# An expert stage rewritten as one flat list of passes, with a turning weight ring and sums kept in PSUM

## What is computed

```python
logits = xf @ w_router + b_router          # 256 tokens, 32 experts
top_v, top_i = lax.top_k(logits, 4)        # 4 experts per token
gates = softmax(top_v)
# for each expert e, on the rows xb of the tokens that chose it:
g = xb @ w_gate[e] + b_gate[e]
u = xb @ w_up[e] + b_up[e]
g = minimum(g, 7.0); u = clip(u, -7.0, 7.0)
glu = g * sigmoid(1.702 * g)
y = ((u + 1.0) * glu) @ w_down[e] + b_down[e]
out[token] += gate * y
# then x + out, and a final rms_norm
```

## Time and profile before

| | |
|---|---|
| time, median of 3 runs | 1571.98 us (1571.66 to 1572.05) |
| span of the profiled execution | 1570.4 us |
| TensorE busy | 1454.5 us, 93% |
| VectorE, ScalarE, GpSimd busy | 502.8, 185.6, 25.1 us |
| moved by DMA | 466 MB, 297 GB/s over the span |
| expert stage, first weight product to last | 546.2 to 1556.9 us |

### The profile page before, as it was taken

How to read it: one execution, slowest core, us unless ns; L and a number is a source line. 1 busy time by engine, 2 the same in 40 slices (tenths; PEclk the granted TensorE clock), 3 DMA queues, 4 the chain that set the end, 5 groups by cost and what they waited for, 6 DMA issues and landing times.

```text
span 1570.4 us, 17757 instructions
## 1 busy us (share of the span) xinstructions
PE 1454.5 (93%) x6407; PEld 656.1 (42%) x6408; DVE 502.8 (32%) x1092; ACT 185.6 (12%) x371; POOL 25.1 (2%) x26
## 2 busy tenths in 40 slices
PE   5999989997988899999999999999999999999896
PEld 4856567664664433333333333333333333333332
DVE  1425424434484421322322322322322322322222
ACT  1212011111160000100100100000000000000001
POOL 0000000001000100000000000000000000000000
PEclk9999989999998699999999999999999999999999
DMA  9722163233520662999999999999999999999291
GB/s 327 275 74 82 54 243 131 68 119 101 193 107 1 238 264 95 381 423 429 428 427 428 430 426 430 427 426 428 430 427 428 427 427 429 429 426 427 111 381 73
DMA packets 61683, 466.04 MB, mean 297 GB/s; under 512 B 6497, under 2 KB 10333, under 8 KB 36957
## 3 DMA queue, kind: packets, MB, share of 16 engines
q1 hardware_dynamic: 58152, 462.78, 71.9%
q0 software_dynamic: 624, 2.10, 0.4%
q10 hardware_dynamic: 2884, 0.87, 0.2%
HBM read 464.68 MB, written 1.05 MB: 297 GB/s over the span
## 4 chain that ended last, share of the span: by engine, by line
issue 79%; PE 17%; DVE 3%; ACT 1%; POOL 1%; DVEq 0%; POOLq 0%
PE bank L710 6%; PE bank L717 5%; PE bank L872 1%; PE bank L1047 1%; PE bank L965 0%; PE bank L918 0%; PE bank L1024 0%; POOL small L453 0%; ACT mem L643 0%; PE bank L1013 0%; PE bank L1060 0%; PE bank L943 0%; PE bank L766 0%; PE bank L788 0%; PE bank L722 0%
## 5 line engine op out<-in xcount | busy, mean ns | idle before, releaser
L1089 PE MATMUL bank<-ring,mem 128*64 128x512 f32 x3264 | 725.0, 596 | 25.1 <-ACT mem L685 22.0
L1089 PEld LDWEIGHTS bank<-ring,mem 128*64 128x64 f32 x3264 | 229.1, 137 | 469.6 <-issue 438.1
L1821 DVE TENSOR_SCALAR mem<-bank 128x512 f32<-128x512 f32 x34 | 23.5, 692 | 505.0 <-PE bank L1096 505.0
L710 PE MATMUL bank<-ring 128*128 128x256 f32 x768 | 168.6, 380 | 1.0 <-DVE ring L1526 1.0
L710 PEld LDWEIGHTS bank<-ring 128*128 128x128 f32 x768 | 145.1, 190 | 22.4 <-DVE ring L1526 1.4
L1833 DVE TENSOR_TENSOR x<-x,bank 128x512 f32<-128x512 f32 x140 | 89.3, 680 | 164.9 <-PE bank L1101 164.9
L717 PE MATMUL bank<-ring 128*128 128x512 f32 (+2 forms) x320 | 124.0, 549 | 3.1 <-DMA ring<-in_w_in_dram 2.0
L717 PEld LDWEIGHTS bank<-ring 128*128 128x128 f32 x320 | 63.3, 200 | 59.6 <-issue 53.0
L1101 PE MATMUL bank<-mem 64*128 64x512 f32 x280 | 78.5, 639 | 3.7 <-ACT mem L679 1.5
L681 ACT ACTIVATE mem<-mem 128x512 f32<-128x512 f32 x32 | 20.1, 629 | 511.9 <-DVE mem L1821 511.9
L1096 PE MATMUL bank<-const,mem 128*64 128x512 f32 x272 | 69.9, 592 | 0.0
(11 more groups left out here) (331 smaller groups left out, 842.5 us busy)
## 6 DMA issues: line engine op xcount, KB each, us to landing
ring<-in_w_gate_dram SPq DMA_DIRECT2D x64, 2048.0 KB, 14.2
ring<-in_w_up_dram SPq DMA_DIRECT2D x64, 2048.0 KB, 12.9
ring<-in_w_down_dram SPq DMA_DIRECT2D x64, 2048.0 KB, 9.0
ring<-in_w_in_dram SPq DMA_DIRECT2D x19, 2048.0 KB, 9.1
ring<-in_w_out_dram SPq DMA_DIRECT2D x6, 2048.0 KB, 7.8
ring<-in_w_in_dram SPq DMA_DIRECT2D x2, 1056.0 KB, 7.4
const<-in_consts_dram SPq DMA_DIRECT2D x1, 1872.0 KB, 7.3
x<-in_x_dram SPq DMA_DIRECT2D x1, 1024.0 KB, 5.2
```

What stands on the lines that cost most here:

```text
L710: i = mm(b[:, S * j:S * j + S], w[:, k, P * (c + j):P * (c + j + 1)], hT[:, k, :], start=(k == 0), stop=(k == KC - 1))
L1089: i = halves(lambda n, at: mm(dst[at, :], lhs[:, c, T * h:T * (h + 1)], w[:, c, 512 * n:512 * (n + 1)], start=(h == 0 and c == 0), stop=(d ...
L1821: i = ts(g_sb, GB[:, :], SWIGLU_LIMIT, None, ALU.min)
```

## The change

All passes are one list, numbered j = expert + extra passes so far. Tables by pass replace those by expert: `of_expert` (which expert pass j belongs to), `slot_at` (each token's place less 64 j) and `slot_gate`, computed before the stage by a few small matmuls. VectorE and ScalarE run one loop over the number of passes, read from `n_total`. TensorE runs over the experts in rounds of four, each with a body for passes that aren't the expert's last and one for the last; both call `expert_block`, and only the last gives slots back. The eight slots turn: load n goes to slot n % 8. Four banks (`OUT`) hold x and collect b_down and all results in PSUM until the end; x is put there by a matmul with the identity. The biases use 32 rows each (gate at partitions 0 to 31, up at 32 to 63) and come first in a pass. Gathered rows share a bank with the gate product, transposed rows with the up product, and h transposed with y.

```diff
-MAIN_STEPS, PRE_STEPS, EX_STEPS = 6, 1, 8
+BLOCK_STEPS = 4
+RING = SLOTS + 2
+RING_EXPERTS = 4
+MAX_BLOCKS = 48
...
-        DB = [bank[0], bank[2], bank[6], bank[7]]
-        GB, UB, YB, XS, XTB, HTB, OB = bank[0], bank[1], bank[2], bank[3], bank[4], bank[5], bank[6:8]
+        OUT = [bank[2], bank[3], bank[6], bank[7]]
+        GXS, UXT, YHT, GTB = bank[0], bank[1], bank[4], bank[5]
...
+            round_turns = RING_EXPERTS * EXPERT_TURNS
+            for n in range(round_turns):
+                if n < RING:
+                    free_before_experts(n)
                 else:
-                    sp.wait_ge(w_used, turn + 1)
+                    sp.wait_ge(w_used, n - RING + 1)
                 sp.sem_inc(load_begun, 1)
+                load_turn(slice(n // EXPERT_TURNS, n // EXPERT_TURNS + 1), n)
+            with sp.Fori(0, E // RING_EXPERTS - 1) as turn:
+                for n in range(round_turns):
+                    sp.wait_ge(w_used, turn * round_turns + (round_turns + n - RING + 1))
+                    sp.sem_inc(load_begun, 1)
+                    load_turn(bass.ds(turn * RING_EXPERTS + (RING_EXPERTS + n // EXPERT_TURNS), 1), n)
...
+            with act.Fori(0, blocks) as j:
+                act.wait_ge(ex["gc"], j + 1)
                 A(tanh_g, g_sb, ACT.Tanh, scale=SWIGLU_ALPHA / 2).then_inc(ex["eg"], 1)
+                act.wait_ge(ex["xs"], j + 2)
+                A(as_chunks(xs_sb), by_chunk(GXS[:, :]), ACT.Copy).then_inc(ex["xs_out"], 1)
+                act.wait_ge(ex["ht"], j + 1)
+                A(hT_sb, YHT[:, :], ACT.Copy).then_inc(ex["ht_out"], 1)
+                act.wait_ge(ex["y"], j + 1)
+                A(y_sb, YHT[:, :], ACT.Copy).then_inc(ex["y_out"], 1)
...
+            def biases():
+
+                for m, dst in enumerate((GXS, UXT)):
+                    of = slice(E * m, E * (m + 1))
+                    i = halves(lambda n, at: mm(dst[at, :], bsel[of, :], bias[of, 512 * n:512 * (n + 1)],
+                                                start=True, stop=False, skip_group_check=True))
                 return i
+
+            def add_up(c):
+
+                return halves(lambda n, at: mm(OUT[2 * c + n][:, :], gT[at, P * c:P * (c + 1)], y_sb[at, :],
+                                               start=False, stop=False, skip_group_check=True))
...
             i.then_inc(out_ready, 1)
+            for c in range(TC):
+                for h in range(2):
+                    mm(OUT[2 * c + h][:, :], ident, x[:, c, 512 * h:512 * (h + 1)], start=True, stop=False,
+                       skip_group_check=True)
             pe.wait_ge(mask_ready, 1)
...
+                pe.wait_ge(ex["xt_out"], j + 1)
+                pe.wait_ge(ex["bsel"], j + 1)
+                biases()
+                used(product(GXS, arrived_turn(0), chunked(xT), 0, False, False))
+                product(GXS, arrived_turn(1), chunked(xT), 1, False, True).then_inc(ex["g"], 1)
+                used(product(UXT, arrived_turn(2), chunked(xT), 0, False, False, used))
+                product(UXT, arrived_turn(3), chunked(xT), 1, False, True).then_inc(ex["u"], 1)
+                pe.wait_ge(ex["gc"], j + 1)
+                pe.wait_ge(ex["sel"], j + 2)
+                gather(used).then_inc(ex["xs"], 1)
+                pe.wait_ge(ex["y_out"], j + 1)
+                pe.wait_ge(ex["gt_out"], j + 1)
+                add_up(0)
+                pe.wait_ge(ex["h"], j + 1)
+                turn4(YHT, h_sb).then_inc(ex["ht"], 1)
+                add_up(1)
+                pe.wait_ge(ex["xs_out"], j + 2)
+                turn4(UXT, xs_sb).then_inc(ex["xt"], 1)
+                pe.wait_ge(ex["ht_out"], j + 1)
+                used(product(YHT, arrived_turn(4), chunked(hT_sb), 0, True, False))
+                product(YHT, arrived_turn(5), chunked(hT_sb), 1, False, True).then_inc(ex["y"], 1)
+                pe.wait_ge(ex["selg"], j + 1)
+                for c in range(TC):
+                    i = tp(GTB[:, P * c:P * (c + 1)], selg[:, c, :], ident)
+                    i.then_inc(ex["gt"], 1) if c else used(i)
+
+            with pe.Fori(0, E // RING_EXPERTS) as turn:
+                for at in range(RING_EXPERTS):
+                    e = turn * RING_EXPERTS + at
                     first = pe.value_load(n_before[0:1, bass.ds(e, 1)], min_val=0, max_val=16)
                     more = pe.value_load(n_more[0:1, bass.ds(e, 1)], min_val=0, max_val=3)
                     with pe.If(more > 0):
                         with pe.Fori(0, more) as b:
...
+                            expert_block(e, e + first + b, turn, at, False)
+                    expert_block(e, e + first + more, turn, at, True)
```

More of the change, by code:

```diff
@@ L392, in _ @@
                     load_cols(turn, ins["w_out_2"][0], 512 * (turn - len(IN2_GROUPS)), 512)
[L395 to L404, removed]
-                else:
-                    sp.wait_ge(out_ready, OUT_0 + OUT_L * DEPTH + turn)
@@ L1130, in _ @@
             pe.wait_ge(ex["sel"], 1)
-            gather(sel).then_inc(ex["xs"], 1)
-            pe.wait_ge(tr_used, tr_n[0])
+            gather().then_inc(ex["xs"], 1)
+            pe.wait_ge(first_ready, 1)
+            b = tr2()
+            for m in range(2):
+                i = mm(b[E * m:E * (m + 1), 0:1], before[0:E, 0:E], blocks_of[0:E, :], start=True, stop=True,
+                       skip_group_check=True)
+            i.then_inc(tr_ready, 1)
+            b = tr2()
+            for c in range(TC):
+                i = tp(b[0:E, P * c:P * (c + 1)], place[:, c, :], ident)
+            i.then_inc(tr_ready, 1)
+            pe.wait_ge(ex["xs_out"], 1)
+            turn4(UXT, xs_sb).then_inc(ex["xt"], 1)
+            pe.wait_ge(tr_used, tr_n[0] - 1)
             pe.wait_ge(bdown_in, 16)
@@ new lines, in _ @@
+            pe.wait_ge(tr_used, tr_n[0])
+            pe.wait_ge(tables_ready, 1)
+            b = tr2()
+            for n, src in enumerate((placeT, gatesT)):
+                for c in range(TC):
+                    o = MAX_BLOCKS * (2 * n + c)
+                    i = mm(b[:, o:o + MAX_BLOCKS], src[:, P * c:P * (c + 1)], of_expert[0:E, :], start=True, stop=True,
+                           skip_group_check=True)
+            i.then_inc(tr_ready, 1)
+            pe.wait_ge(tr_used, tr_n[0])
@@ L1227, in _ @@
+            pe.wait_ge(ex["gt_out"], blocks + 1)
+            for c in range(TC):
+                add_up(c).then_inc(ex["out"], 1)
         @block.vector
@@ new lines, in _ @@
+            b = tr2()
+            tr2_done(v.tensor_copy(gatesT, b[0:E, 0:S]))
+            b = tr2()
+            first = b[0:2 * E, 0:1]
+            st.go(v.tensor_copy(block_0, first))
+            st.go(tt(block_1, blocks_of, first, ALU.add))
+            tr2_done(ts(slot_0, first, float(T), None, ALU.mult))
+            st.wait()
+            v.wait_ge(tr_used, n_tr[0])
+            blocks = iota[:, 0:MAX_BLOCKS]
+            st.do(ts(of_expert, blocks[0:2 * E, :], block_0, None, ALU.is_ge))
@@ L1794, in _ @@
+            st.wait()
+            v.sem_inc(ex["bsel"], 1)
+            st.go(v.memset(y_sb, 0.0))
+            st.go(v.memset(gT, 0.0))
+            st.do(ts(nblk, totals, float(T), None, ALU.is_gt))
+            for b in range(2, S // T):
+                st.do(stt(out=nblk, in0=totals, scalar=float(T * b), in1=nblk, op0=ALU.is_gt, op1=ALU.add))
             st.do(v.tensor_tensor_scan(ncum, ones[:, 0:E], nblk, 0.0, ALU.mult, ALU.add))
@@ L1811, in _ @@
[L1811 to L1823 removed]
+            tables = b[:, 0:4 * MAX_BLOCKS].rearrange("p (n c j) -> p n c j", n=2, c=TC)
@@ new lines, in _ @@
+            st.go(stt(out=slot_at, in0=blocks.unsqueeze(1).to_broadcast([P, TC, MAX_BLOCKS]), scalar=-float(T),
+                      in1=tables[:, 0, :, :], op0=ALU.mult, op1=ALU.add))
+            tr2_done(ts(slot_gate, tables[:, 1, :, :], 0.5, None, ALU.mult))
+            st.wait()
+            v.wait_ge(tr_used, n_tr[0])
+            v.wait_ge(count_ready, 3)
+            v.sem_inc(ex["gt_out"], 1)
+            blocks = v.value_load(n_total[0:1, 0:1], min_val=E, max_val=MAX_BLOCKS - 1)
+            st_main = st.base + st.n
```

372 lines of the change are left out of this document (123 added, 249 removed).

## The result

The changed kernel takes 1616.8 us (median, 1613.8 to 1617.1) where the kernel before takes 1571.8: a ratio of 1.0284, 95% interval 1.0271 to 1.0298. It is slower by 45 us, where I had forecast 1529 us and a range up to 1590.

What follows compares the result with a forecast made beforehand. TensorE paces the old kernel; after the change transfers lead. Expert 29's effective start at 1406.7 plus four passes of 27.5 gives 1516.7; an 11.2 us end makes a 1528 span, forecast 1529 us; range 1521 to 1590.

Steps and rivals of the forecast that it cites:

- Rival 1: TensorE's longer loop is refetched each round, 60 blocks taking DMA engine time: 37 to 69 us, about 1582 us; chance 0.36.
- the loop that stays: Forecast case: TensorE's eight-body expert loop is kept without refetch, 10 to 16 instruction blocks, 1529 us; chance 0.40.
- loops of six blocks: Layer loops of 1456 records, six 16 KB instruction blocks, replay without refetch in the old profile; nine blocks not shown.
- A pass without waits, 27.5 us: One expert-stage pass on TensorE falls from 29.42 us to 27.5 (27.4 to 28.7), through removed waits and faster biases.
- Both old waits: TensorE's waits in a pass for VectorE's product, 0.60 us, and ScalarE's copy, 0.69 us, both go: 1.29 us less.
- The bias group of eight records: Four bias halves of a pass all run at once on 32-row tiles: 1.06 us plus 0.1, saving 0.56 us.
- The transfers then lead at 29.4 us: In the expert stage six slots need 29.40 us of DMA against TensorE's 27.5, so TensorE waits for slots.
- First pass 552 us: Expert stage's first pass starts at 552 us, 546 to 556, after added early matmuls and table products.
- Load after expert 1's passes 611.7: Load 14 goes out at 611.7 us, after expert 1's last pass does its first product; DMA then never stops.
- Expert 29 in effect at 1406.7: Expert 29's pass starts in effect at 1406.7 us, set by its fourth slot's landing 14.7 us after the first.
- 11.2: Tail from the expert stage's end to the span's end: 11.2 us, where the old kernel has 13.5.

Runs made afterwards that it cites:

- e2: Changed kernel with ring of eight slots and four-expert loop kept, but one body per expert, repeated for further blocks (four bodies in the loop): 1527.7 us, ratio 0.9727.
- e5: e2 with three quarters of each expert load left out, instructions the same: 1490.4 us, ratio 0.9482.
- e15: e2 with eight experts in a round instead of four, no jumps over bodies: 1533.3 us, ratio 0.9758, 52 instruction blocks.
- e16: e2 with sixteen experts in a round instead of four: 1532.1 us, ratio 0.9750, 47 instruction blocks.
- e13: e1 with one never-executed body behind the first expert only, five bodies in the loop: 1535.0 us, ratio 0.9769, 16 instruction blocks.
- e9: e1 with one never-executed body behind each expert, six bodies in the loop: 1838.0 us, ratio 1.1691, 152 instruction blocks.
- e8: e1 with one never-executed body behind its first expert and two behind its second, seven bodies: 1842.0 us, ratio 1.1716, 152 instruction blocks.
- e7: e5 with both biases on one group of 32 rows, so two products run side by side, not four: 1518.9 us, ratio 0.9666.
- e1: Changed kernel with TensorE's loop put back to two experts (four bodies) and the old slot scheme: 1536.1 us, ratio 0.9770, 14 instruction blocks.
- e14: e13 with a never-executed half body behind the second expert, five and a half bodies: 1533.9 us, ratio 0.9764, 16 instruction blocks.
- e6: Changed kernel with three quarters of each expert load left out, instructions the same: 1568.2 us, ratio 0.9988.

## Why the prediction was wrong, point by point

**The steps that failed: the sum had no refetch, and the rival that had one put the stops under the wait for slots.** The sum that gives 1529 us holds no term for fetching the loop again; that alone is worth the 89 us by which e2, which meets that sum within 1.3 us, differs from the changed kernel. Rival 1 had the mechanism: nine blocks a round on a loop that is not kept, 70 or more blocks, under 428 GB/s on the ring, over 31 us an expert. The profile shows 96 blocks, dips to 363 GB/s, and 31.7 us an expert (126.8 / 4). But it put the price on the transfers, 0.61 to 1.15 us of an engine for each of 60 blocks, and said "Stalls of TensorE at the jump back are under the wait for slots". They are not, or only in part. TensorE had 27.3 us of work against 29.4 of transfers, so 2.1 us a pass or 8.4 us a round of cover; the branch back, the further boundary and the half clock behind them take 17.6, as the timeline of the round above shows. Eight rounds of the difference are an estimate of 74 of the 89 us; over the whole stage e5 puts the cover at 37.4 us and the refetch at 126.5. No wait for the ring shows on TensorE in the changed kernel's stage. The price that I did put in, of the blocks' share of the engines, is not what costs: e15 and e16 bring 37 and 32 blocks more than e2 for 5.6 and 4.4 us.

**The chance.** I gave the loop that stays 0.40 and its loss 0.36. What spoke for the first were loops of six blocks that replay; they say nothing of nine. The Trainium skill (Runtime: NRT & Kernel Launch, Instruction fetch mechanics), with its 128 KiB, spoke against it, and the loop of eight bodies is indeed not kept. How large the kept loop may be in bytes stays open. e16 brings 15 blocks of 16 KB in 400 us of straight code, in which 14.3 passes run (27.30 us each to about 890 us, 29.4 behind), an estimate of 16.8 KB a body; by it five and a half bodies (92 KB) are kept and six (101 KB) are not, less than those 128 KiB. By the 11 blocks that come for a round of eight bodies, as I had counted for e13, a body is 22 KB, and the same step lies between 121 and 132 KB; but such a round has jumps and may fetch a block more than once. What is measured is the step between five and a half and six bodies.

**The number of blocks.** I had 60 from load 14 on, about nine a round; the changed kernel brings 82 more than the one before, 11 a round. e9 and e8 were missed by a count of that kind.

**A pass without waits, 27.5 us.** 27.30 us in the changed kernel (576.56 to 603.86) and in e2. Both old waits are gone. The bias group of eight records takes 1.09 us, where I took 1.16. With two products side by side it takes 0.84 us more (e7), 1.93 us, where I had 2.2: all four do run side by side.

**The transfers then lead at 29.4 us.** Right for a kernel that stays loaded: e2 waits from 911.9 us on, its passes 29.4 us apart, at 428 GB/s.

**Start and end of the stage.** First pass 552 us: it begins at 545.4 in e2 at half clock, so in effect at 548.7 (the next at 576.01, less 27.30). Load after expert 1's passes 611.7: 608.1. Expert 29 in effect at 1406.7: 1404.7 (the next pass at 1432.0, less 27.3). Four passes of 27.3 and 11.1 us to the end of the span, 1525.0, where I had 11.2 (a slip in its last term, four of 0.68 being 0.2 and not 0.1 above 2.48, does not show). Each is 2 to 4 us early, as the start is. All of it holds in e2 and none of it shows in the changed kernel.

**Two edits costed at nothing, the register loads and the branch over the unused body at each pass's start:** they cost nothing while the code is kept (e1, e14), and are the places of the stops once it is not.

Not tested alone: the sums in PSUM, the order of the list, and the ring of eight apart from the one body (e1 against e2, 8.4 us, holds both). Why one stop of 2 to 3 us is followed by the lower clock and another is not stays open.

## What to carry to other kernels

Before a loop is unrolled further, count its code against what its engine keeps, jumped-over branches included: here a second copy of the body, run twice in 34 passes, took the whole gain and more. Write the rare case as another turn of the same body. When a stall is put "under" a wait elsewhere, write both down in us a round and subtract; mine was 17.6 against 8.4. Where the stops were fewer, in e15, most of them did go under the wait.

## What the runs showed of the hardware

- The step is sharp: from five and a half bodies in the loop to six, bodies that never run counted, 304 us at once, 19 us for each of 16 rounds.
- Code that runs straight on is fetched at no visible cost even with the DMA engines at 100%: passes at 27.30 us with about a block each. In the loops that are not kept TensorE stops at a branch, and again a few instructions behind its target (1.72 us inside a pass of the changed kernel, 4.04 in e9). At a pass boundary of the changed kernel and of e15 it is 2.6 to 3.9 us for one branch, 7.4 to 7.9 at the branch back of the changed kernel, both under full transfers, and 1.9 to 3.2 us with the engines at a third (e6).
- Stops of 3.9 and 7.9 us were followed by 6 us with the granted clock at 0.52 to 0.54, the lower of the two levels; of those of 2 to 3 us some were (0.51 for 3.6 us behind the 2.13 us of e6) and some were not (1.00 behind its 2.63 us). In e15 from 797.0 to 803.0 us:

```profile
793.00:797.04 4.04, 0.18 (x2) 0.03 (x1) 1.36 (x5) 0.46 (x1) 0.00 (x0) 0.86 1.00 422
797.04:803.00 5.96, 5.96 (x18) 1.54 (x20) 0.00 (x0) 0.00 (x0) 0.00 (x0) 0.52 1.01 426
803.00:827.10 24.10, 24.10 (x114) 8.06 (x111) 3.84 (x6) 2.08 (x4) 0.00 (x0) 1.00 1.01 427
```
